# Key products move to GpSimd, and narrow matmuls pair up in halves of the array

## The reference

```python
z = p + (p_prev - p) * mu
r, k, v, zw, za, zg = _split(z, RWKV_SPLITS)
w_logit = (w0 + jnp.tanh(zw) @ w2).astype(f32)          # rank 64
decay = jnp.exp(-jnp.exp(-jax.nn.softplus(-w_logit) - 0.5))
a = jax.nn.sigmoid((a0 + za @ a2).astype(f32))          # rank 64
kk = _l2norm(k * hp(k_k))
k = k * (1.0 + (a - 1.0) * hp(k_a))
# step: sa = state @ -kk_t; state = state * w_t + sa * (kk * a)_t + v_t * k_t
...
q, k, v, gate, b, a = _split(p, GDN_SPLITS)             # b, a: 6 columns each
beta = jax.nn.sigmoid(b.astype(f32))
g = -jnp.exp(a_log.astype(f32)) * jax.nn.softplus(a.astype(f32) + dt_bias.astype(f32))
```

## Time and profile before

| | |
|---|---|
| median of 3 runs | 1101.14 us (1097.43 to 1104.62) |
| the profiled execution | 1106.6 us, its span 1104.7 us |
| TensorE busy | 1023.0 us, 93% of the span |
| VectorE busy | 575.3 us, 52% |
| ScalarE busy | 478.6 us, 43% |
| GpSimd busy | 61.2 us, 6%, in 73 instructions |
| chain that ended last | TensorE 74%, VectorE 9%, ScalarE 7%, issue 5%, GpSimd 1% |
| mean granted TensorE clock | 0.947 of full |

### The profile page before, as it was taken

One profiled execution on the slowest core, in us unless ns is written; L12 is line 12 of the kernel. 1 busy time (PEld: TensorE's weight loads), 2 busy tenths in 40 slices (PEclk: granted clock), 3 DMA queues, 4 the chain that ended last, 5 costly groups with the idle time before them and its releaser, 6 DMA issues.

```text
span 1104.7 us, 17427 instructions
## 1 busy us (share of the span) xinstructions
PE 1023.0 (93%) x7463; PEld 914.1 (83%) x7463; DVE 575.3 (52%) x854; ACT 478.6 (43%) x707; POOL 61.2 (6%) x73
## 2 busy tenths in 40 slices
PE   3899999999989879999997899997999888999998
PEld 3899997887668779999986896876878688999887
DVE  3575444444546645555544658366453435666444
ACT  4553334445554354443334473435424324555332
POOL 0000000110002300000000200012220000000000
PEclk9999999999999989999999699998969589999999
DMA  8974542232435524544535141221000023544541
GB/s 316 165 272 172 209 154 77 86 143 96 160 144 205 194 77 153 201 180 166 216 122 207 60 153 44 110 102 53 2 1 3 1 109 120 198 184 177 205 153 38
DMA packets 12796, 149.89 MB, mean 136 GB/s; under 512 B 1632, under 2 KB 1760, under 8 KB 4016
## 3 DMA queue, kind: packets, MB, share of 16 engines
q1 hardware_dynamic: 10224, 139.12, 34.0%
q0 software_dynamic: 1264, 5.24, 2.8%
q10 hardware_dynamic: 1232, 4.42, 1.0%
HBM read 144.59 MB, written 4.19 MB: 135 GB/s over the span
## 4 chain that ended last, share of the span: by engine, by line
PE 74%; DVE 9%; ACT 7%; issue 5%; POOL 1%; ACTq 0%; POOLq 0%; DVEq 0%
PE bank L575 55%; PE bank L544 3%; PE bank L1187 3%; DVE ARENA L1863 2%; PE bank L707 1%; ACT W_HIGH L1355 1%; DVE W_LOW L1822 1%; DVE RING_LOW L1947 1%; POOL HN L2560 1%; PE bank L558 1%; ACT GATE_HIGH L1389 1%; PE bank L967 1%; ACT ARENA L1482 1%; PE bank L1202 1%; DVE X L2057 1%
## 5 line engine op out<-in xcount | busy, mean ns | idle before, releaser
L1822 DVE TENSOR_TENSOR W_LOW<-weights,W_HIGH 128x2048 fp32r<-128x2048 f32 (+1 forms) x109 | 249.1, 2285 | 267.1 <-ACT W_HIGH L1355 267.1
L1355 ACT ACTIVATE W_HIGH<-weights 128x2048 fp32r<-128x2048 f32 (+1 forms) x109 | 207.3, 1902 | 323.7 <-PE bank L575 323.7
L575 PE MATMUL bank<-OVER_HT,W_HIGH 128*128 128x256 f32 x608 | 172.5, 284 | 2.1 <-DVE OVER_HN L1835 2.1
L575 PE MATMUL bank<-OVER_HN,W_HIGH 128*128 128x256 f32 x608 | 172.1, 283 | 0.0
L575 PE MATMUL bank<-OVER_HT,W_LOW 128*128 128x256 f32 x608 | 172.1, 283 | 0.0
L575 PEld LDWEIGHTS bank<-OVER_HT,W_HIGH 128*128 128x128 f32 x608 | 116.4, 191 | 2.7 <-issue 2.7
L575 PEld LDWEIGHTS bank<-OVER_HN,W_HIGH 128*128 128x128 f32 x608 | 116.4, 191 | 0.0
L575 PEld LDWEIGHTS bank<-OVER_HT,W_LOW 128*128 128x128 f32 x608 | 116.4, 191 | 0.0
L575 PE MATMUL bank<-W_LOW,HID_HIGH 128*128 128x512 f32 x216 | 84.0, 389 | 0.0
L575 PE MATMUL bank<-W_HIGH,HID_LOW 128*128 128x512 f32 x216 | 84.0, 389 | 0.0
L575 PE MATMUL bank<-W_HIGH,HID_HIGH 128*128 128x512 f32 x216 | 84.0, 389 | 0.0
(11 more groups left out here) (421 smaller groups left out, 2056.6 us busy)
## 6 DMA issues: line engine op xcount, KB each, us to landing
weights<-weights_dram SPq DMA_DIRECT2D x63, 2048.0 KB, 8.6
bias_rows_dram<-ARENA POOLq DMA_DIRECT2D x1, 3072.0 KB, 39.5
BIAS<-params_dram ACTq DMA_DIRECT2D x1, 1997.0 KB, 11.5
weights<-weights_dram SPq DMA_DIRECT2D x1, 1664.0 KB, 6.8
weights<-weights_dram SPq DMA_DIRECT2D x1, 1584.0 KB, 8.4
weights<-weights_dram SPq DMA_DIRECT2D x1, 1536.0 KB, 8.1
X<-x_dram ACTq DMA_DIRECT2D x1, 1024.0 KB, 9.8
HT<-bias_rows_dram POOLq DMA_DIRECT2D x1, 1024.0 KB, 8.5
```

Of the source, the lines that this page charges most:

```text
L575: ins = pe.matmul(o, left[a][k], right[b][k], start=(first and k == 0 and a + b == 0), stop=(last and k == n - 1 and a == 1))
L1355: act.activation(piece_parts(k)[0], piece_source(k), ACT.Copy).then_inc(sem("pieces_high"), 1)
L1822: dve.tensor_tensor(low, piece_source(k), high.bitcast(F32), ALU.subtract)\
```

## The change

Three edits that do not need each other.

First, the low rank products run in pairs: the two halves of the array (pb 0 and 64) alternate, into two banks opened together. The fills ("lora", 0) to ("lora", 3) now are w2's tiles 0 and 1, a2's tiles 0 and 1, w2's tile 2, a2's tile 2, and ScalarE empties them in this order.

Second, the two runs of gate matmuls become eight pairs: the second row of each pair goes to output partitions 32 to 37, the same bank columns as the first. As it now lies on other partitions than GAX and its bias, VectorE copies it first, waits for the copy (link), and adds the bias in place.

Third, the products A3 = KK * A3, KK = KK * E3 and A3 = A3 * E3 move from VectorE to GpSimd, all three ahead of the two products that it had. The semaphores alpha_ready and rw_factors are now GpSimd's.

```diff
--- before.py
+++ after.py
@@ -892,12 +892,14 @@
             pe.wait_ge(sem("stream_by_pool"), 1)
 
             pe.wait_ge(sem("lora_by_act"), 1)
-            for n, (pb, tiles) in enumerate(((0, (0, 1)), (0, (2,)), (HD, (0, 1)), (HD, (2,)))):
-                o = open_fill(("lora", n))
+            for n, tiles in enumerate(((0, 1), (2,))):
+                banks = open_halves(("lora", 2 * n), ("lora", 2 * n + 1))
                 for j, t in enumerate(tiles):
-                    ins = pe.matmul(o[:, j * S:(j + 1) * S], prm2("w2a2", t * P, P)[pb:pb + HD, :],
-                                    LO[pb:pb + HD, 0, :], start=True, stop=True)
-                close_fill(ins)
+                    for pb, o in zip((0, HD), banks):
+                        ins = pe.matmul(o[:, j * S:(j + 1) * S], prm2("w2a2", t * P, P)[pb:pb + HD, :],
+                                        LO[pb:pb + HD, 0, :], start=True, stop=True)
+                        if t == tiles[-1]:
+                            close_fill(ins)
             pe.wait_ge(sem("lora_by_dve"), 1)
             for o, t, last in tile_slots([("rw_g", 0), ("rw_g", 1)]):
                 ins = pe.matmul(o, prm2("g2", t * P, P), LO[:, 1, :], start=True, stop=True)
@@ -921,8 +923,10 @@
             close_job(ins)
             close_job(product_f(open_job(("in2", 3, 1))[:, 0:S], w, 2 * P))
             o = open_job(("in2", 3, 2))
-            for t in range(2):
-                ins = product_f(o[0:RH, t * S:(t + 1) * S], w, 384 + RH * t, RH)
+            for k in range(KD):
+                for t, pb in enumerate((0, 32)):
+                    ins = pe.matmul(o[pb:pb + RH, 0:S], w[:, k, 384 + RH * t:384 + RH * (t + 1)], HT[:, k, :],
+                                    start=(k == 0), stop=(k == KD - 1))
             close_job(ins)
 
             pe.wait_ge(sem("mla_qk_ready"), 1)
@@ -1616,7 +1620,7 @@
             shift_tiles(2, 0, (4, 5))
             shift_tiles(2, 1, (6, 7))
 
-            for n, (dst, bias, tiles) in enumerate(((LW, "w0", (0, 1)), (LW, "w0", (2,)), (A3, "a0", (0, 1)), (A3, "a0", (2,)))):
+            for n, (dst, bias, tiles) in enumerate(((LW, "w0", (0, 1)), (A3, "a0", (0, 1)), (LW, "w0", (2,)), (A3, "a0", (2,)))):
                 o = fill_arrived(act, ("lora", n))
                 for j, t in enumerate(tiles):
                     ins = act.activation(dst[:, t, :], o[:, j * S:(j + 1) * S], ACT.Tanh, scale=0.5, bias=prm2(bias, t))
@@ -2238,7 +2242,8 @@
             shift_tiles(3, 0, (8, 9))
             shift_tiles(3, 1, (10,))
             o = job_arrived(dve, ("in2", 3, 2))
-            dve.tensor_scalar(GAX, o[0:RH, S:2 * S], prm2("g_dtb")[0:RH, :], None, ALU.add)
+            link(dve.tensor_copy(GAX, o[32:32 + RH, 0:S]))
+            dve.tensor_scalar(GAX, GAX, prm2("g_dtb")[0:RH, :], None, ALU.add)
             job_out(dve.tensor_copy(BETA, o[0:RH, 0:S]), ("in2", 3, 2))
             wait_job_out(dve, ("in2", 3, 2))
             dve.sem_inc(sem("beta_in"), 1)
@@ -2289,10 +2294,6 @@
             for name, a, b in ((("kk_r", 0), 0, 2), (("kk_r", 1), 2, 3)):
                 o = fill_arrived(dve, name)
                 fill_out(dve.tensor_tensor(flat(KK[:, a:b, :]), flat(KK[:, a:b, :]), o[:, 0:(b - a) * S], ALU.mult), name)
-                wait_fill_out(dve, name)
-            dve.tensor_tensor(A3[:, :, :], KK[:, :, :], A3[:, :, :], ALU.mult)
-            dve.wait_ge(sem("decay_exp"), 1)
-            dve.tensor_tensor(KK[:, :, :], KK[:, :, :], E3[:, :, :], ALU.mult).then_inc(sem("alpha_ready"), 1)
             convs(8, 12)
             convs(12, 16)
 
@@ -2300,8 +2301,6 @@
                 o = fill_arrived(dve, name)
                 fill_out(dve.tensor_tensor(flat(BON[:, a:b, :]), o[:, 0:(b - a) * S], flat(V3[:, a:b, :]), ALU.mult),
                          name)
-            dve.wait_ge(sem("decay_exp"), 3)
-            dve.tensor_tensor(A3[:, :, :], A3[:, :, :], E3[:, :, :], ALU.mult).then_inc(sem("rw_factors"), 1)
             conv_taps(16)
             conv_out(16)
             dve.wait_ge(sem("gg_tanh"), 1)
@@ -2586,7 +2585,14 @@
             pool.wait_ge(sem("masks_by_pool"), 3)
 
             pool.wait_ge(sem("rw_squares"), 2)
+            wait_fill_out(pool, ("kk_r", 0))
+            wait_fill_out(pool, ("kk_r", 1))
+            pool.tensor_tensor(A3[:, :, :], KK[:, :, :], A3[:, :, :], ALU.mult).then_inc(sem("gains_by_pool"), 1)
+            pool.wait_ge(sem("decay_exp"), 1)
+            pool.wait_ge(sem("gains_by_pool"), 1)
+            pool.tensor_tensor(KK[:, :, :], KK[:, :, :], E3[:, :, :], ALU.mult).then_inc(sem("alpha_ready"), 1)
             pool.wait_ge(sem("decay_exp"), 3)
+            pool.tensor_tensor(A3[:, :, :], A3[:, :, :], E3[:, :, :], ALU.mult).then_inc(sem("rw_factors"), 1)
             pool.tensor_tensor(K3[:, :, :], K3[:, :, :], E3[:, :, :], ALU.mult)
             pool.tensor_tensor(R3[:, :, :], R3[:, :, :], GM[:, :, :], ALU.mult).then_inc(sem("factors_by_pool"), 1)
             pool.wait_ge(sem("factors_by_pool"), 1)
```

## The result

| | before | after |
|---|---|---|
| median | 1103.48 us (9 runs, 1097.43 to 1106.93) | 1109.61 us (9 runs, 1104.93 to 1114.32) |
| ratio | | 1.0048, 95% interval 1.0027 to 1.0068 |
| profiled execution | 1106.6 us, span 1104.7 us | 1110.02 us, span 1108.0 us |

The change costs 0.48% of 1103.5, that is 5.3 us (3.0 to 7.5 us by the interval); the two medians lie 6.1 us apart. The forecast was +3.95 us and 1105.1 us, in a range of 1098.5 to 1111.5 us. The median of before over nine runs lies 2.3 us above that of the three from which the forecast started, so +3.95 us on it would be 1107.4 us.

The account below looks back on a forecast made before the run. The start of the convolutions, behind VectorE and ScalarE, was taken to bound the middle stage, not TensorE's work. -0.3 + 2.0 + 1.4 + 0.85 = +3.95 us on a 1101.14 us median gave 1105.1 us, range 1098.5 to 1111.5 us.

Parts of the forecast that it names:

- Low rank products, 0: Low rank products: pairs take about half of 2.10 us, but ScalarE's table load ends the wait either way; 0.
- Gate rows, -0.3 us: Gate rows: pairs save TensorE 3.4 us, but the path through VectorE to the tanh gains only 0.3 us.
- all of VectorE's wait: Gate rows: the term's most favourable bound, -0.7 us, if VectorE's whole wait for the rows were gained.
- First two products, +2.0 us: Key products: two GpSimd products of 1.81 us each delay ScalarE's exponential from 724.06 to 726.05 us.
- Third product, +1.4 us: First convolution taps: a third GpSimd product there holds a third VectorE tap, 1.91 instead of 0.48 us.
- The third rival: Key products and taps: GpSimd alone is quicker and the third tap isn't held; +0.9 us, 1102 us, chance 0.09.
- What VectorE sheds, 0: Convolutions: taking the products off VectorE gains nothing; the third's 0.95 us was covered by the wait for ScalarE.
- TensorE's waits behind it: Behind the key products: about 4 us remains ahead of the squares, about 3.5 us appears ahead of the last projection job; hidden.
- Clock in the attention stage, +0.85 us: Attention scores: a longer TensorE wait may drop its clock; middle between no fall and 1.7 us.
- the prediction's own sign: Wrong in size if a granted clock of 0.50 appears where it was 1.00, or goes where it was 0.50.
- The first rival: Around 860 to 894 us: half-clock stretches shift, one fewer; not slower, 1099.6 us, chance 0.2.
- The second: Second rival: further clock drop in the last projection job or products behind longer waits; +4 + 5.5, 1110.6 us, chance 0.13.

Follow-up runs that it names:

- e4_lora: Kernel before with only the low rank products paired; median 1105.59 us, ratio 0.9995.
- e3_pool: Kernel before with only the three key products moved from VectorE to GpSimd; median 1106.85 us, ratio 1.0017.
- e5_pool_two: Kernel before with only the first two key products moved to GpSimd, the third left on VectorE; median 1106.54 us, ratio 1.0041.
- e1_gate: Kernel before with only the gate rows paired, computed once; median 1113.82 us, ratio 1.0044, 8 of 12 runs above 1111.5 us.
- e6_pool_third: Kernel before with only the third key product moved to GpSimd; median 1104.74 us, ratio 1.0025.
- e12_gate_later: e1_gate plus two extra unused VectorE products in the key chain, making later stages 2 us later; median 1105.76 us, ratio 1.0013.
- e11_gate_lora: Kernel before with gate and low rank pairs, without the GpSimd move; median 1115.10 us, ratio 1.0069, 9 of 12 runs above 1111.5 us.
- e7_vector: Kernel before with all five key products on VectorE, none on GpSimd; median 1102.12 us, ratio 1.0000.
- e8_vector_pairs: e7_vector plus low rank pairs and gate pairs computed twice; median 1103.04 us, ratio 1.0010.
- e9_gate_vector: e7_vector plus gate pairs computed once; median 1104.68 us, ratio 0.9985, no run above 1111.5 us.

## Why the prediction was right, and where it was not

**Low rank products, 0.** Right (e4_lora 0.9995). The pairs take 1.57 us, not half of 2.10 us, and TensorE then waits 2.17 us for ScalarE, where the earlier trace rows have 1.63 us. The wait took the gain whole. That the pairs would take about half was wrong, and cost nothing.

**Gate rows, -0.3 us.** TensorE's part was right: 3.63 us for 3.4, though the row it was taken from the earlier trace rows shows pairs in the two halves of the array's columns, and not at output partitions 0 and 32. Against the one profile that the prediction had, the scores do come 0.25 us earlier (S 31.98 for 32.23). Against the five others the path's part has the wrong sign: +0.5 us. The step that failed is the bound "all of VectorE's wait". That wait of 0.72 us existed only because TensorE was late in this one execution: it had been at half clock in 662 to 664 us. In five profiles with unchanged gate rows and full clock there, VectorE does not wait for them. In before the MLA transposes start 28.55 us behind the low rank products, in e3_pool, with the same instructions up to there, 26.86 us. Nothing was there to be gained, and the extra instruction was left as a cost. The prediction had the clock row and the wait row side by side and did not join them.

**First two products, +2.0 us.** Right: +1.94 us in after (C 4.98 for 3.04), the same in e3_pool and e5_pool_two. (Its upper bound is +2.4 by its own sum, not +2.5.) Each took 1.81 us, the first started 0.17 us behind VectorE as read, the second 0.14 us behind the first, and ScalarE 0.03 us behind that. The bound of two cheap products is excluded: with no VectorE instruction beside it, GpSimd needs 1.81 us too. The GPSIMD Engine Reference of the Trainium skill (section "Elementwise — side-by-side cycle accounting") led to an estimate of 1.69 us; the row is 0.12 us dearer.

**Third product, +1.4 us.** Right: the six taps went from 5.27 us in e1_gate and e4_lora's 5.28 us to 6.61 us, D grew by 1.3 us, and e5_pool_two and e6_pool_third tie it to this product alone. The third rival, which wanted this term at 0, falls with it. "The two alternate, one tap for one product" is now shown by three counts of products beside six taps, 0, 2 and 3, with 2.95, 5.2 and 6.6 to 6.7 us. The Trainium skill (SBUF — State Buffer, section "SBUF: two separate sides") says that a VectorE instruction with two SBUF inputs and a GpSimd instruction that reads SBUF lock a shared port pair against each other: whichever starts first has it for its whole length. The trace agrees: a tap of 0.48 us takes up to 1.91 us beside products of 1.81 to 1.99 us.

**What VectorE sheds, 0.** Right: e6_pool_third takes the third product off VectorE, and D grows by just what the taps lose.

**TensorE's waits behind it.** A new wait of about 3.5 us was foreseen ahead of the last projection job. It is 2.38 us, and another of 0.59 us stands ahead of the job before it, which the prediction had missed. At the attention it had 1.5 us ahead of the transposes and 3.3 us ahead of the scores; they are 3.13 and 1.91 us. The wait ahead of the squares is 3.98 us, as before. None of it is on the path.

**Clock in the attention stage, +0.85 us.** The mechanism appears, but the change did not bring its cost. Stretches of after behind the gate rows and ahead of the scores:

```profile
682.00:684.00 2.00, 2.00 (x11) 1.91 (x10) 1.92 (x6) 0.00 (x0) 0.00 (x0) 0.50 1.07 451
...
688.00:690.00 2.00, 2.00 (x7) 1.61 (x6) 1.15 (x6) 1.29 (x5) 0.00 (x0) 0.55 0.00 0
```

The MLA transposes at 681.68 us take 3.45 us behind a wait of 3.13 us; in e4_lora they take 1.95 us. That part is hidden behind ScalarE. Behind the scores, AB less S is 33.01 us in after against 31.32 us in before: +1.7 us, the upper bound. But the five profiles with unchanged gate rows have 33.01 us as well. Ten microseconds with the first scores or the products behind them, in before (scores at 689.70 us) and in e4_lora (682.41 us):

```profile
690.00:700.00 10.00, 10.00 (x57) 8.92 (x56) 2.61 (x14) 4.07 (x12) 0.00 (x0) 1.00 0.27 115
680.00:690.00 10.00, 7.59 (x31) 6.47 (x32) 1.81 (x10) 3.52 (x11) 0.00 (x0) 0.83 0.45 185
```

In e4_lora TensorE, on time at the gate rows, waits 2.57 us ahead of the scores, and the clock is 0.50 in 684 to 686 us. In before it came late, waited 1.73 us, and the clock stayed at 1.00. So the fall that the prediction feared behind a longer wait is what the unchanged code does in five of six profiles; before's profile was the exception. Against the five the term is 0 in after and 1.9 us in e1_gate and e12_gate_later (34.9 us), where the clock is 0.50 for some 10 us around the scores and falls once more ahead of the keys. Together with the gate rows, the prediction had +0.55 us up to the key products; against the five profiles (64.42 us in the mean) after has +0.57 us. That sum agrees by luck: a gain of 0.3 that was a loss of 0.5, and a clock term of 0.85 that was 0. By the prediction's own sign it was wrong in size: a granted clock of 0.50 appears in 682 to 684 us, where it had been 1.00, and is gone behind the low rank products.

**The sum.** 0.57 + 1.94 + 1.34 = 3.85 us in the stage against the five profiles, for 3.95 us predicted. The measured 5.3 us (3.0 to 7.5 us) holds it. The remaining 1.4 us have no row of their own.

**The first rival** (a half-clock stretch less) did not come. **The second** (more half clock further on, +5.5 us) is what the gate pairs do alone: 8 and 9 runs of 12 are long. Its mechanism was right and its place was wrong: not the last projection job or the products behind it, but the first matrix inversions. In the whole change only 2 of 9 runs lie above 1111.5 us (1112.2 and 1114.3 us, clock 0.943 and 0.942), and its runs do not fall in two groups. It differs from e11_gate_lora by the GpSimd move alone, which costs 3.3 us in its stage and takes nearly all the long runs away (2 of 9 for 9 of 12), as e12_gate_later's delay of 2 us does. That the shift is the reason is argued from that likeness. By ratios gate and low rank pairs together cost 0.69% and the GpSimd move 0.17%, which would make 0.86%; all three cost 0.48%. That gap of 0.38% is less than the three half-widths combined as independent errors (0.42%), so that the parts do not add rests on the counts of long runs, and not on the ratios. The prediction treated its terms as independent, and for the clock they are not.

**A better version** was looked for in e7_vector, e8_vector_pairs and e9_gate_vector. All shorten the stage by 2.3 us, and none is measurably faster than the kernel before.

## What to carry to other kernels

Cost a product that moves to a slower engine by who waits for it, and count what it does to the other engine's instructions beside it: here 1.9 us of the one and 1.3 to 1.4 us of the other, each right to 0.1 us from rows of the trace before. Before a wait in one profile is counted as a gain, look whether the waited-for engine was at full clock in that execution; a second profile of the same code settles it. Taking work from TensorE in front of a wait bought nothing here, though it is busy for 93% of the span, and it brought half-clock stretches later. Such a cost shows in how the single runs fall in groups, not in the median alone.

## What the runs showed that I had not expected

The same stretch of code with the matrix inversions takes 130 to 136 us in twelve profiles and about 145 us in two, a shift of 2 us in a stage before it goes with the difference (e1_gate, e12_gate_later), and one kernel goes both ways: e1_gate at 1101.5 to 1102.8 us and at 1113.1 to 1120.0 us, with mean granted clocks of 0.947 to 0.952 and 0.928 to 0.939. In the long runs that were profiled, TensorE stands at 1.2 of 2.4 GHz nearly throughout (0.50 to 0.55 granted) for almost 40 us in which its rows show it busy throughout. A granted clock of 0.50 there makes it look busier (20.00 of 20 us, for 17.89 us before), not idler.
